# Moving VectorE's operands into PSUM, spreading the decays, and rounding weights earlier in a two-layer kernel

## The reference

```python
# first layer
z = rms_norm(x, norm_g) @ w_in
q, c_kv, q_idx, k_idx, w_idx, g_attn, x_rnn, g_rnn, merge = split_cols(z)
s_idx = relu(einsum('btjd,bsd->btjs', q_idx, k_idx)); s_idx = einsum('btjs,btj->bts', s_idx, w_idx)
_, idx = lax.top_k(where(causal, s_idx, -inf), 64)
o = softmax(q_lat . c_sel - slope * dist) . c_sel            # 16 heads, then w_uv
y_attn = (o * silu(g_attn)) @ w_attn_proj
u = causal_depthwise_conv(x_rnn, conv_w, conv_b)             # 4 taps
r, i = sigmoid(u @ w_a + b_a), sigmoid(u @ w_x + b_x)        # blocks of 64
a = exp(-8 * r * softplus(-lam)); b = sqrt(1 - a**2) * (i * u)
h = associative_scan(h = a * h + b)
y_rnn = (h * silu(g_rnn)) @ w_rnn_proj
x = rms_norm(x + (sigmoid(m_a) * y_attn + sigmoid(m_r) * y_rnn) @ w_out, final_g)
# second layer
proj = rms_norm(x, attn_norm) @ w_in_2                       # c_q, c_kv, k_r, q_b, k_b, v_b, gates
x = x + (sigmoid(g_a) * mla(c_q, c_kv, k_r) @ w_o_mla + sigmoid(g_b) * moba(q_b, k_b, v_b) @ w_o_moba) @ w_out_2
x = x + moe(rms_norm(x, ffn_norm)); out = rms_norm(x, final_norm)
```

## Time and profile before

| | |
|---|---|
| runs | 736.65, 736.76, 737.17 us, median 736.76 |
| the profiled execution | 739.29 us, span 737.4 us, granted clock 0.98 |
| TensorE matmul | busy 662.7 us (90%), 5600 matmuls |
| VectorE | busy 397.5 us (54%) |
| ScalarE | busy 327.3 us (44%) |
| POOL | busy 394.2 us (53%), all of it before about 500 us |
| HBM | 179.73 MB read |

### The profile page before, as it was taken

How to read it: one execution, slowest core, us unless ns; L and a number is a source line. 1 busy time by engine, 2 the same in 40 slices (tenths; PEclk the granted TensorE clock), 3 DMA queues, 4 the chain that set the end, 5 groups by cost and what they waited for, 6 DMA issues and landing times.

```text
span 737.4 us, 13811 instructions
## 1 busy us (share of the span) xinstructions
PE 662.7 (90%) x5600; PEld 553.8 (75%) x5600; DVE 397.5 (54%) x672; ACT 327.3 (44%) x599; POOL 394.2 (53%) x284
## 2 busy tenths in 40 slices
PE   3999989989999999989999999999999986786763
PEld 3999879889989999988779999999655443443321
DVE  6799954699995247997955655533322111111102
ACT  7556657855653456564358755451211110011003
POOL 3889657687879989798799665881000000000000
PEclk9999999999999999999999999998999998899997
DMA  8755333433444555434364434999799999999992
GB/s 346 276 171 173 115 114 124 160 119 122 165 122 165 179 196 196 171 127 161 115 216 132 154 128 148 374 424 384 287 424 419 423 418 424 420 421 422 421 417 85
DMA packets 26130, 181.72 MB, mean 246 GB/s; under 512 B 2896, under 2 KB 3152, under 8 KB 4688
## 3 DMA queue, kind: packets, MB, share of 16 engines
q1 hardware_dynamic: 25488, 179.22, 63.6%
q10 hardware_dynamic: 576, 1.57, 0.6%
HBM read 179.73 MB, written 1.05 MB: 245 GB/s over the span
## 4 chain that ended last, share of the span: by engine, by line
PE 46%; DVE 25%; DMA 16%; ACT 5%; issue 4%; POOL 2%; SPq 2%; ACTq 0%; DVEq 0%
PE D L446 25%; DMA big<-w_expert_dram 7%; DVE big L1440 6%; PE L L881 4%; DMA ring<-w_expert_dram 4%; DMA attn<-w_expert_dram 4%; POOL ring_r L1423 2%; DVE small L1440 2%; SPq L387 2%; PE L L861 2%; PE QB L914 2%; DVE hT L1440 2%; PE L L603 2%; DVE big_r L1459 1%; DVE big_r L1464 1%
## 5 line engine op out<-in xcount | busy, mean ns | idle before, releaser
L1423 POOL TENSOR_TENSOR ring_r<-ring,ring_r 128x512 fp32r<-128x512 f32 x280 | 394.0, 1442 | 105.3 <-ACT ring_r L1030 105.2
L446 PE MATMUL D<-scr_r,ring_r 128*128 128x256 f32 x1104 | 213.1, 289 | 0.8 <-DVE big L1440 0.8
L1030 ACT ACTIVATE ring_r<-ring 128x1024 fp32r<-128x1024 f32 x140 | 146.2, 1053 | 75.7 <-PE D L446 68.5
L446 PEld LDWEIGHTS D<-scr_r,ring_r 128*128 128x128 f32 x1104 | 175.4, 191 | 3.4 <-issue 2.1
L446 PE MATMUL D<-hT_r,ring_r 128*128 128x256 f32 x552 | 156.1, 283 | 0.0
L446 PE MATMUL D<-big_r,ring_r 128*128 128x256 f32 x1110 | 138.5, 285 | 1.6 <-POOL ring_r L1423 1.6
L446 PEld LDWEIGHTS D<-big_r,ring_r 128*128 128x128 f32 x1110 | 135.0, 192 | 3.7 <-issue 2.8
L446 PEld LDWEIGHTS D<-hT_r,ring_r 128*128 128x128 f32 x552 | 105.8, 192 | 1.2 <-issue 1.0
L1440 DVE SCALAR_TENSOR_TENSOR th<-th,L 64x256 f32<-64x256 f32 x32 | 13.4, 418 | 136.6 <-ACT th L1345 136.0
L1345 ACT ACTIVATE th<-L 64x256 f32<-64x256 f32 x16 | 6.0, 377 | 91.8 <-PE L L881 91.8
L881 PE MATMUL L<-big,small 128*32 128x256 f32 x432 | 33.3, 412 | 12.3 <-DMA big<-w_expert_dram 9.3
(11 more groups left out here) (358 smaller groups left out, 1011.7 us busy)
## 6 DMA issues: line engine op xcount, KB each, us to landing
ring<-w_dense_dram SPq DMA_DIRECT2D x69, 1024.0 KB, 4.9
big<-w_expert_dram SPq DMA_DIRECT2D x40, 1024.0 KB, 26.3
ring<-w_expert_dram SPq DMA_DIRECT2D x30, 1024.0 KB, 26.5
wu<-w_expert_dram SPq DMA_DIRECT2D x6, 1024.0 KB, 25.3
scr<-w_expert_dram SPq DMA_DIRECT2D x5, 1024.0 KB, 21.8
hT<-w_expert_dram SPq DMA_DIRECT2D x5, 1024.0 KB, 23.9
attn<-w_expert_dram SPq DMA_DIRECT2D x5, 1024.0 KB, 24.1
xT<-w_expert_dram SPq DMA_DIRECT2D x5, 1024.0 KB, 26.0
```

What stands on the lines that cost most here:

```text
L446: last = mm(out_, r32(w[i][ws]), r32(x[j][xs_]), start=start and m == 0, stop=stop and m == 2)
L1030: A_(r32(hi_unit(j)), dense_unit(j), ACT.Copy).then_inc(hi_ready, 1)
L1423: last = g.tensor_tensor(r32(w), w, r32(h).bitcast(F32), ALU.subtract)
```

## The change

Eight edits:

1. `first_chunk`: the pass with the weights' rest comes before the pass with the activations' rest.
2. Index scores: the relu is written back into its PSUM bank, and VectorE reads it there. TensorE waits for `idx_acc` instead of `idx_relu` before it overwrites a bank. The latent norm moves from before the index scores to behind the mask.
3. Convolution: bias, last tap and running sum lie in PSUM (`CB`: banks QB, UB, L0, L1) and the last tap's result goes to `u`. So all gates wait for the whole convolution (`conv_done` 8), and are laid out differently: two after `q` chunk 5, then one after each third of chunks 6 and 7.
4. Attention in both layers: bias, maximum and exponential stay in L0 and L1; VectorE normalises from there into `E`. `S` is gone. A score pair waits for the probabilities of the pair before (`probs`) instead of for `biased`.
5. Attention output: `gated_out` works in place in PSUM, and `split_out` and `head_split` split from there (`split_bank`); `head_out` and `o_ready` are gone, and TensorE waits for the split (`lo_of`).
6. The decays are spread in pieces of one to three chunks over the first two pairs, the squares come in the third; the odd recurrence step stands between the two gates of a pair.
7. ScalarE rounds three units further before and within the split of `hT` of the second layer, and one unit earlier at each pair of `uq`.
8. Units of `uq` are rounded and subtracted over 768 columns only (`width`).

```diff
+        CB = [QB, UB, L0, L1]
...
+        def width(n):
+
+            return QC * P if 0 <= n - UNIT0["uq"] < H2 else UNIT
...
+                if between:
+                    for k in range(kc):
+                        last = mm3(dst, w, src, np.s_[:, k * P:(k + 1) * P], np.s_[:, k, :], k == 0, k == kc - 1)
+                        if k in (2, 5):
+                            between(k // 3)
+                    last.then_inc(unit_done, 1)
+                    between(2)
+                    return
...
+                pe.wait_ge(lo_ready, 1)
+                for k in range(DC):
+                    mm(dst, r32(w[1][:, k * P:(k + 1) * P]), r32(x0_hi[:, k, :]), start=False, stop=False)
                 for k in range(DC):
                     pe.wait_ge(lo_of["x0"], k + 1)
-                    mm(dst, r32(w[0][:, k * P:(k + 1) * P]), r32(x0_lo[:, k, :]), start=False, stop=False)
...
-                        pe.wait_ge(idx_relu, j - 2)
+                        pe.wait_ge(idx_acc, j - 2)
...
-                pe.wait_ge(conv_done, c + 1)
-                pe.wait_ge(idx_relu, IDXH)
+                pe.wait_ge(conv_done, 8)
...
-                chunk("q", c, h2)
+                chunk("q", c, h2, between=(lambda i: rg_gates(3 * c - 16 + i)) if c >= 6 else None)
...
-                if c >= 6:
-                    for i in range(4 * (c - 6), 4 * (c - 6) + 4):
-                        rg_gates(i)
+                if c == 5:
+                    rg_gates(0)
+                    rg_gates(1)
...
-                pe.wait_ge(biased, a) if a else pe.wait_ge(gates, 8)
+                pe.wait_ge(probs, a) if a else pe.wait_ge(gates, 8)
...
-                    pe.wait_ge(o_ready, a // 2 - 1)
+                    o_bank_emptied(a // 2 - 1)
...
-                    last = A_(u[:, c, :], bank[:, m * T:(m + 1) * T], ACT.Identity, bias=V("conv_b", c),
-                              scale=V("conv_w", 3 * 8 + c))
+                    last = A_(CB[i][:, m * T:(m + 1) * T], bank[:, m * T:(m + 1) * T], ACT.Identity,
+                              bias=V("conv_b", c), scale=V("conv_w", 3 * 8 + c))
...
-                    A_(scores_in[:, j % 4, :], IB[j % 4][:, 0:CAUSAL], ACT.Relu).then_inc(idx_relu, 1)
+                    A_(IB[j % 4][:, 0:CAUSAL], IB[j % 4][:, 0:CAUSAL], ACT.Relu).then_inc(idx_relu, 1)
...
-                    last = A_(E[:, a % 2, c0:c0 + n], S[:, a % 2, c0:c0 + n], ACT.Exp,
+                    last = A_(LB[a % 2][:, c0:c0 + n], LB[a % 2][:, c0:c0 + n], ACT.Exp,
...
             keys_in(0)
+            decays(0, 2)
...
+                    if m == 2:
+                        decay_squares()
...
+                if m < 2:
+                    decays(2 + 3 * m, 4 + 2 * m)
                 if m < H1 // 2:
                     side_gate(2 * m + 1)
-                if m < 2:
-                    decays(4 * m, 4 * m + 4)
...
+                if m < 2:
+                    decays(4 + 2 * m, 5 + 3 * m)
...
-            round_pieces("att2", hT, scr, lambda i: act.wait_ge(normed, NM0[N_FIN1] + 2 * i + 2))
+            advance(UNIT0["cq"] + 5 + HI_UNITS)
+
+            def hidden_ready(i):
+
+                if i:
+                    advance(UNIT0["cq"] + 5 + min(i, 2) + HI_UNITS)
+                act.wait_ge(normed, NM0[N_FIN1] + 2 * i + 2)
+
+            round_pieces("att2", hT, scr, hidden_ready)
...
             for i in range(4):
+                advance(UNITS_AT[FILL0["uq"] + i] - 1 + HI_UNITS)
                 act.wait_ge(unit_done, UNITS_AT[FILL0["uq"] + i])
...
+                taps = CB[c // 2][:, (c % 2) * T:(c % 2 + 1) * T]
                 for t in (2, 1, 0):
-                    ins = stt(u[:, c, :], xr[:, c, 1 + t:1 + t + T], V("conv_w", t * 8 + c), u[:, c, :],
+                    ins = stt(taps if t else u[:, c, :], xr[:, c, 1 + t:1 + t + T], V("conv_w", t * 8 + c), taps,
...
+                if a >= 2:
+                    dve.wait_ge(pt_mm, a - 1)
                 for tt, (c0, n) in enumerate(tiles):
-                    last = v.tensor_scalar(E[:, a % 2, c0:c0 + n], E[:, a % 2, c0:c0 + n],
+                    last = v.tensor_scalar(E[:, a % 2, c0:c0 + n], LB[a % 2][:, c0:c0 + n],
...
-                stt(oT[:, n, :], o_bank(n)[:, 0:T], 0.5, sg[:, n, :]).then_inc(o_ready, 1)
+                step(stt(o_bank(n)[:, 0:T], o_bank(n)[:, 0:T], 0.5, sg[:, n, :]))
+
+            def split_bank(name, lo, hi, i, bank):
+
+                v.tensor_copy(r32(hi[:, i, :]), bank).then_inc(hi_of[name], 1)
+                dve.wait_ge(hi_of[name], i + 1)
+                v.tensor_tensor(r32(lo[:, i, :]), bank, r32(hi[:, i, :]).bitcast(F32), ALU.subtract).then_inc(lo_of[name], 1)
...
-                    if 2 <= m < 7:
-                        lru(2 * m - 3)
+                        if f % 2 == 0 and 2 <= m < 7:
+                            lru(2 * m - 3)
```

More of the change, by code:

```diff
@@ L288, in build @@
         logits, biased, maxed, expd, probs = [sem(n) for n in ("logits", "biased", "maxed", "expd", "probs")]
[L289 removed]
+        pt_mm, pt_ready, o_mm = [sem(n) for n in ("probs_transposed", "pt_ready", "o_matmul")]
         mixed = sem("mixed_ready")
@@ L453, in open_bank, with chunk @@
                 return DB[f % 2]
-            def chunk(stage, c, src, kc=DC, split=None, per=2):
+            def chunk(stage, c, src, kc=DC, split=None, per=2, between=None):
                 bank = open_bank(stage, c // 2) if c % 2 == 0 else DB[(FILL0[stage] + c // 2) % 2]
@@ L613, in transposes, with o_bank_emptied @@
                 last.then_inc(pt_mm, 1)
+            def o_bank_emptied(n):
+                for name, size in (("o", 8), ("ob", 4), ("oa", 4)):
+                    if n <= size:
+                        break
+                    n -= size
+                pe.wait_ge(lo_of[name], n)
             def pv_pair(a, v_of):
@@ L682, in _ @@
             chunk_pair("cq", x1, "x1")
-            pe.wait_ge(o_ready, 8)
+            pe.wait_ge(lo_of["o"], 8)
             pe.wait_ge(rooted, N_FIN1)
@@ L811, in route @@
                 if i == 0:
-                    pe.wait_ge(o_ready, 16)
+                    pe.wait_ge(lo_of["oa"], 4)
                 for c in (2 * i, 2 * i + 1):
@@ L1145, in _ @@
             v1_in(3)
-            for c in range(4):
+            for c in range(7):
                 rg_tanh(c)
             q_in(3)
-            for c in range(4, 8):
-                rg_tanh(c)
+            rg_tanh(7)
             act.wait_ge(gates, 8)
@@ L1420, in _ @@
                 for half in range(2):
-                    cols = np.s_[:, half * UNIT // 2:(half + 1) * UNIT // 2]
+                    cols = np.s_[:, half * width(n) // 2:(half + 1) * width(n) // 2]
                     w, h = dense_unit(n)[cols], hi_unit(n)[cols]
```

59 lines of the change are left out of this document (22 added, 37 removed).

## The result

| | before | after |
|---|---|---|
| median of runs, us | 736.96 (736.65 to 738.35, 4 runs) | 727.52 (726.98 to 729.1, 4 runs) |
| profiled execution, us; its span | 739.29; 737.4 | 727.65; 725.9 |

The ratio is 0.9869, with a 95% interval of 0.9854 to 0.9884: 8.5 to 10.8 us shorter. Forecast were 726.1 us and a gain of 10.7, from 736.76, the median of the first three runs of before. The sum came nearly true; several of its terms did not.

What follows compares the result with a forecast made beforehand. Experts are bound by transfers that start at TensorE's counts, so TensorE's waits in the dense layers set the end: 1.4 + 1.8 + 5.2 + 0 + 2.6 - 0.3 = 10.7 us, 736.76 to 726.1 us; 8-in-10 range 722.5 to 731.5.

Steps and rivals of the forecast that it cites:

- First chunk: First chunk: matmuls with the weights' rest fill TensorE's 1.7 us wait for VectorE; gain 1.4 us, between 0.9 and 1.7.
- Index scores and convolution: Before the first attention: PSUM operands end index heads near 50 us, convolution at 81, so TensorE's gate waits shrink.
- Gain 1.8: Recurrence gates: of TensorE's waits of 1.4 + 0.9 us all but about 0.5 go; bounds 0 and 2.8.
- First attention: First attention: PSUM normalisation and spread decays remove waits of 2.8 + 1.6 + 0.8; gain 5.2 us, bounds 3 and 5.7.
- Second norm: Second norm: earlier roundings help POOL but slow VectorE's products into `hT`; gain 0, bounds 2.5 won and 1.5 lost.
- the end of the pair at 323.9: Chunk pair behind the second norm: expected to end at 323.9 us, where it ended before the change.
- rival (a): Second norm gets its wait back, POOL ahead and VectorE not slowed: 2.5 us more, 723.6 us; chance 0.09.
- Rival (b): VectorE's 6 us lateness at the second norm reaches rotations (2 to 3 us); 1.5 lost at the pair: 730 to 731; 0.16.
- `uq`: `uq` products: 768-column units and earlier rounding take back 2.6 of 2.9 us lost; bounds 0 and 2.9.
- Second attention: Second attention: only the first pair costs, ScalarE being late with copies; 0.3 us lost, bounds 0 and 2.
- Rival (c): Second attention's eight score pairs wait for the normalised heads, making the kernel slower: 741 us; chance 0.04.
- Rival (d): The change does nothing because the transfers set the end by themselves: 736.8 us; chance 0.03.

Runs made afterwards that it cites:

- before_start: Kernel before with only the first chunk's new order (weights' rest ahead of the input's rest): 735.24 us, ratio to before 0.9977.
- keys_free: Changed kernel with the first keys product and first attention chunk ahead of the wait for the last `q` copy: 726.44 us, ratio to before 0.9852.
- before_spread: Kernel before with only the decays in pieces, their squares and the recurrence step moved: 731.06 us, ratio to before 0.9921.
- exps_sbuf: Changed kernel with exponentials written to SBUF and normalised there; bias and maxima stay in PSUM: 727.1 us, ratio to before 0.9873.
- decays_old: Changed kernel with decays, squares and recurrence step back in their old places: 729.07 us, ratio to before 0.9907.
- decays_sbuf: Changed kernel with decays, squares and recurrence step in old places and exponentials written and normalised in SBUF: 731.95 us, ratio to before 0.993.
- warm: Changed kernel with 32 unused matmuls in TensorE's wait ahead of the second norm's chunk pair: 726.12 us, ratio to before 0.9852.
- norm_plain: Changed kernel without the extra weight roundings at the second norm: 725.05 us, ratio to before 0.9846.
- full_uq: Changed kernel with `uq` units of 1024 columns again and no rounding ahead of each `uq` copy: 730.4 us, ratio to before 0.9921.
- both_mended: Changed kernel with the edits of `norm_plain` and `keys_free` together: 723.05 us, ratio to before 0.9815.
- mended_fourth: `both_mended` with one weight rounding ahead of the fourth piece of the hidden state at the second norm: 723.26 us, ratio to before 0.9818.

## Why the forecast came out near, step by step

**First chunk**, forecast 1.4: right. 1.4 us by the traces, 1.4 by `before_start`. The wait for VectorE of 1.7 us is gone; one of 0.7 us for GpSimd, which the forecast did not have, stands in its place.

**Index scores and convolution.** The prices and times were right (0.49 us a tap, ends at 50.0 and 79.9), and so were the gates' waits: 0.7 us is left of 2.3. What failed was the step "Gain 1.8": it came out as 0.1, because the wait for the last `q` copy, which the gates had hidden, appeared as 1.8 us at the keys. `keys_free` gives them back at that place (1.9 us).

**First attention**, forecast 5.2, measured 5.8. Size right, reason wrong in its weights. I had named the 3 us per pair that VectorE saves and the pieces of the decays side by side, as if both were needed. `before_spread` shows that the pieces (with squares and recurrence step) alone end all the waits and bring the whole 5.8; `exps_sbuf` that the exponentials' home changes nothing beside them; `decays_old` and `decays_sbuf` that the homes are a second cover, worth 4 of the 5.8 us only where the decays are not spread, and at least 1.8 of it is the exponentials' home. The chain there was ScalarE's (its copy of the probabilities), and the earlier trace rows say so: two of the three rows name ACT. In the trace of before eight decays of 0.6 us stand in one block (113.84 to 118.4) directly ahead of such a copy, and eight more with the four squares behind the next pair (128.43 to 135.1).

**Second norm**, forecast 0, bound 1.5 lost; measured 2.8 lost. The step that failed is the end of the pair at 323.9: on the old time scale it was 319.28 + 7.3 = 326.6. The 1.4 us per product were right, and the first rest came at 310.67 + 7.3 = 318.0, even before my 318.7. But TensorE waited for the bank copy, which ScalarE makes only after the fourth rounding (311.32 to 311.90), and started at 311.95, which is 319.2 on the old scale. Then the pair's 48 matmuls took 7.3 us, as the clock had fallen; I had left 5.2 us for them, and even at 0.12 us they take 5.8 (`warm`: 311.97 to 317.82). The term had neither the copy nor the clock in it. Before they took 6.5 with a wait for GpSimd inside. So 2.0 us are a longer wait and 0.8 the pair's. Leaving the roundings out is worth 2.3 us in the trace and 2.5 by the medians (`norm_plain`); rival (a) needed products that GpSimd does not hold up, and with the roundings ahead it holds up all eight.

**Rotations.** Not in the sum; the traces differ by 1.5 us there. Most of it is not the change's: from the first swap to the first `uq` products the profiled execution of before needs 18.9 us, `before_start` and `before_spread`, with the same code there, 18.0 each, the changed kernel 17.4. Their waits at the third swap are 0.4 and 0.3 us, that of before 1.3. So 0.6 us is the change's; `full_uq`, which has a wait of 0.33 us there, puts most of it with the `uq` edits. Rival (b) had it the other way round, but its 1.5 us at the pair were there, and more. Its lateness of 6 us did not reach the rotations, and not because VectorE waits for roots, as I had argued: it was made up before them, by the eight products into `xT` at 4.2 us instead of 11.4.

**`uq`**, forecast 2.6: measured 2.6 in the traces, 2.5 to 2.9 by `full_uq`.

**Second attention**, forecast -0.3: measured -0.5, a wait of 0.4 us for the normalised probabilities at the second pair. Rival (c) did not come.

The sum of the pieces is 1.4 + 0.1 + 5.8 - 2.8 + 1.5 + 2.6 - 0.5 = 8.1 us at 450 us, against 10.7 forecast; the profiled executions end 11.6 us apart, since that of before needed some 3 us more from the second attention's end on (granted clock 0.83 in 500 to 520 us, 1.00 after). The medians, 9.4 apart, lie between. The largest errors, 2.8 at the norm and 1.7 at the gates, have one sign; 0.6 in the attention, 1.5 at the rotations and the start of the experts went the other way. No part of the reasoning led to these gains, so that it is partly luck that the forecast was within 1.4 us. Rival (d) is out with any gain at all.

**Left open.** What in bias, maxima and outputs in PSUM makes up the rest of the homes' cover was not tried. From the last product of the second attention to the end the profiled executions take 269.1 to 271.7 us, that of before 273.9, in ways that no edit explains (the scatter of one kernel's runs is as large), so that differences under 1 us between medians are not read here. With the same code at the pair, its length varied from 7.3 to 8.1 us in the six profiles with the longer wait; that of the changed kernel was among the shortest.

## What to carry to other kernels

When work is moved away, ask what the next instruction of the same engine waits for, even where the list of waits shows nothing: the moved work may have hidden it (1.8 us here). When two engines share a lock, giving one its work early takes time from the other. Here the sum stayed the same and only the place of the loss moved, so ask which of the two the bound engine waits for next. And undo a change both ways, alone from before and alone from after: a cover that is there twice looks worthless in one direction and whole in the other.

## Of the hardware, not expected

The same standstill of TensorE does not always come before a fall of the clock. Behind a wait of 2.5 us it stayed up in the profiles of the kernel before and of `before_start`, and fell in `before_spread`, whose code there is the same. Stretches in and behind the wait, first `before_start`:

```profile
315.70:320.00 4.30, 3.82 (x30) 3.65 (x31) 4.30 (x4) 2.27 (x5) 4.30 (x4) 1.00 0.46 191
```

then `before_spread`:

```profile
313.20:317.00 3.80, 3.74 (x19) 3.77 (x20) 3.80 (x4) 2.29 (x5) 3.80 (x3) 0.55 0.48 198
```

It fell in `norm_plain` and `both_mended` too, and stayed up in `mended_fourth` (all 2.5 us), so three times each; in the six profiles with 4.5 us of standstill, that of the changed kernel among them, it fell every time. It can also fall behind less: at the gates, where waits of 0.7 and 1.4 us follow each other, it was 0.56 in 98 to 101 us in `before_spread` and 1.00 in the kernel before, with the same waits. Behind 2.5 us a fall made the pair 7.1 to 7.3 us long instead of 6.5, in which TensorE waits 0.4 us for GpSimd; behind 4.5 us 7.3 to 8.1 instead of the 5.8 of `warm`. That is as much as some edits here bring: one profile is not enough to compare them by. The Trainium skill (TensorE: Matmul & The Clock Gate, "What's actually happening") says as well that the number of slow matmuls differs between runs of one kernel; these rows agree.
